# Storing loaded keys and values from SBUF instead of copying them from HBM to HBM, and building the constant masks on chip

## The chip, the cores and the metric

The kernel runs on one core of a Trainium2 chip. The metric is the device time of one launch in microseconds (us), as the median of several runs. The engines are TensorE (PE; its weight loads are shown as PEld), VectorE (DVE), ScalarE (ACT), GpSimd (POOL) and SyncE (SP). All DMA work is issued from the instruction streams of SP (DMA queue q1) and ACT (queue q10), and both queues run on the same 16 DMA engines.

## The reference, cut to what matters

One decoder layer with two parallel mixers: dilated window attention (8 heads of 64) and a gated convolution of width 3. It runs on 512 prompt tokens and on 64 sample tokens (8 sequences of 8), the latter with a cache of 2048 past keys and values per sequence.

```python
proj = jnp.einsum('btd,de->bte', x, w_in)            # 1024 -> 4096
q, k, v, g_att, gb, gc, hh, g_conv = jnp.split(proj, ...)
k_all = jnp.concatenate([k_past, k], axis=1)         # same for v
# three branches (window, dilation): (128,1), (512,4), (2048,16), merged by their softmax sums
att = o_att * jax.nn.silu(g_att)
u = gc * hh
z = gb * conv3(u) * jax.nn.silu(g_conv)
out = jnp.einsum('bte,ed->btd', concat([att, z]), w_out)
y = _layer_norm(2 ** 0.25 * x + out, ln_g, ln_b)
new_k = k_all[:, n_all - keep:]                      # same for v: the caches are outputs too
```

So the kernel returns y and, beside it, the whole key and value caches, shifted by 8 positions. The shift is done outside; the kernel must bring every cached key and value from its input tensor to an output tensor. Of 2048 cached positions of a sequence 1280 are used by some branch ("used": `k_used`, `v_used`), the other 768 are only handed on ("rest": `k_rest`, `v_rest`).

## The kernel before

All matrix products run on TensorE in fp32r, each product in three passes: the weights and the activations are split into a high and a low part (`w_hi`, `w_lo`, `x_hi`, `x_lo`). ACT makes the high part (`split_hi`, L497), DVE the low part (`split_lo`, L810).

The projection has 32 weight tiles of 128 output features (numbers 0 to 31). A tile is projected in two halves, 256 tokens into the bank `pj_a` and 320 into `pj_b` (L1178 to L1180, 24 matmuls each). Tiles 0 and 1 arrive with the input. Tile n from 2 on is loaded by SP (`load_w`, 512 KB in rows of 4 KB) into one of two slots of `w_raw`; the load waits until DVE has split tile n - 2.

Work goes in four rounds, i = 0 to 3, one for each pair of heads. A round has eight tiles (the last has five): C, H, B and G_CONV of the convolution, then V of the next pair, a gate, and q and k of the next pair. Between the tiles stands the attention of pair i: for the prompt, scores (L1282), mask on DVE (L879), exp on ACT (L603), normalisation (L894), transposes on PE (L1299), copies out of PSUM by ACT (`move_prompt`, L609), products with the values (L1313). For the samples, the same with the used keys from `k_buf` (four slots of 1280 KB, rows of 10 KB, loaded by `load_k`, read by PE at L1333) and the used values from `v_buf` (five slots of 1024 KB, rows of 8 KB, `load_v`, read at L1367). After the rounds comes the output projection (L1492 to L1526) and the layer norm.

Every engine runs an instruction stream written out by hand, in order, with semaphore waits. The ones that matter here:

- SP: `load_w`, `load_k`, `load_v`, `save_v`, `save_k` in a fixed order. In round 0 the order is `load_k(0, 2)`, `load_k(0, 3)`, `save_k(0)`, `load_w(6)`, `load_v(0, 0)`, `load_w(7)`, `load_v(0, 1)`, `load_v(0, 2)`, `load_w(8)`, and so on. Tile 6 is the tile B of round 0.
- ACT: `act_round(i)`. Between its computations stand calls of `copy_next()`. Each issues one copy from HBM to HBM: first the 24 pieces of the rest, then 17 pieces of the used values, then the 16 pieces of the used keys, 57 in all. `short_runs` gives them rows of 4 KB (rest and values) or 5 KB (keys), and 256 rows each. None of them waits for anything.
- SP also stores three pieces of the used values of the last round from `v_buf` (`store_values`, L407), since they are there when the engine has time.
- DVE: `dve_round(i)`. In each round `split_lo` of the tile t0 + 3 (tile 6 in round 0) stands ahead of the last two taps of the convolution and of the third prompt mask.

The masks (`mask_pr`, 128 x 512, and `mask_s`, 128 x 1344) are constants that are loaded whole at the start. `w_out` is loaded into SBUF space that `k_buf`, `v_buf` and the small attention buffers have used before (`load_wo`, in the last round), and so are the residual rows `x_res` (`load_res`).

Of the kernel before, what the change touches and what calls it, by code (L numbers as in the profile page):

```python
# [7 lines left out]
P = 128  # L8
D_MODEL = 1024
SEQ = 512  # L10
# [19 lines left out]
NPAIR = DEC_BATCH // 2  # L30
# [10 lines left out]
S_COLS = USED + NS  # L41
K_PIECES = 4
# [5 lines left out]
N_COPIES = 2 * REST_ROWS + NPAIR * (K_PIECES + V_LOADS) - len(STORED)  # L48
# [31 lines left out]
SAMPLE_AT = 3  # L80
Y_SLOTS = 3
# [12 lines left out]
def layer_step(nc, d):  # L94

    with ExitStack() as ctx:
# [68 lines left out]
        v_in = [sem(f"v_in{n}") for n in range(V_LOADS)]  # L165
        k_saved, v_saved, vn_saved, copied, conv_out = (
# [3 lines left out]
        blank = sem("blank")  # L170
# [118 lines left out]

        block = ctx.enter_context(nc.Block())  # L290

        @block.sync
        def _(sp):
# [93 lines left out]
            sp.wait_ge(k_used, pieces + 2)  # L387
            load_wo(1)
            load_v(NPAIR - 1, 3)
            sp.wait_ge(k_used, pieces + 3)  # L390
            load_wo(2)
            load_v(NPAIR - 1, 4)
            sp.wait_ge(k_used, pieces + 4)
            load_wo(3)
# [55 lines left out]
            sp.wait_ge(copied, 16 * N_COPIES)  # L450
            sp.wait_ge(v_stored, 16 * len(STORED))

        @block.gpsimd
        def _(pool):
            pool.memset(q_bd[:, :], 0.0).then_inc(zeroed, 1)
            pool.memset(u_pad[:, 0:2], 0.0).then_inc(zeroed, 1)
            pool.wait_ge(zeroed, 2)
            pool.wait_ge(small_in, 80)
# [24 lines left out]
            pool.wait_ge(ln_in, 16)  # L483
            pool.partition_broadcast(ln_g[:, :], y_t[0:1, 0:D_MODEL]).then_inc(ln_spread, 1)
            pool.partition_broadcast(ln_b[:, :], y_t[0:1, D_MODEL:2 * D_MODEL]).then_inc(ln_spread, 1)

        @block.scalar
        def _(act):
# [44 lines left out]
            def copy_v(i, s):  # L533
                rows = slice((V_LOADS * i + s) * P, (V_LOADS * i + s + 1) * P)
                act.dma_start(short_runs(d["v_used_out"][rows, :]), short_runs(d["v_used"][rows, :]))\
                    .then_inc(copied, 16)

            copies = iter(range(N_COPIES))

            def copy_next():  # L540

                n = next(copies)
                if n < 2 * REST_ROWS:
                    copy_rest(n)
                elif n < N_COPIES - NPAIR * K_PIECES:
                    n -= 2 * REST_ROWS
                    copy_v(n // (V_LOADS), n % (V_LOADS))
                else:
                    n -= N_COPIES - NPAIR * K_PIECES
                    copy_k(n // K_PIECES, n % K_PIECES)  # L550
# [127 lines left out]
            def act_round(i):  # L678
                t0 = tile0(i)
                copy_c(i, 0)  # L680
                copy_next()
# [25 lines left out]
                copy_next()  # L707
                if i == 1:
                    copy_next()
# [5 lines left out]
                copy_next()  # L715
# [6 lines left out]
                copy_next()  # L722
# [3 lines left out]
                copy_next()  # L726
                split_hi(t0 + 9)
                out_sample(i)

            def act_last_round(i):  # L730
                t0 = tile0(i)
                copy_c(i, 0)
                copy_next()
                out_sample_turned(i - 1)
                exp_prompt(i, 0)
                copy_c(i, 1)
                move_prompt(i, 0)
                exp_prompt(i, 1)
                split_hi(t0 + 2)
                move_prompt(i, 1)  # L740
                exp_prompt(i, 2)
                split_hi(t0 + 3)
                copy_next()
                move_prompt(i, 2)
                exp_sample(i)
                split_hi(t0 + 4)
# [3 lines left out]
                copy_next()  # L750
# [19 lines left out]
                copy_next()  # L770
                out_sample(i)
                copy_next()
                copy_next()
                split_mix(2)
                copy_next()
# [11 lines left out]
            for t in range(QT + 1):  # L787
# [8 lines left out]
                if t < 3:  # L796
                    copy_next()
# [6 lines left out]
        def _(dve):  # L804
# [66 lines left out]
            dve.wait_ge(small_in, 80)  # L871
# [301 lines left out]
        def _(pe):  # L1173
# [16 lines left out]
            def turn_v(i):  # L1190

                if i == 0:
                    pe.wait_ge(pj_read[0], 2)
                    pe.wait_ge(small_in, 80)
# [345 lines left out]
def mask_arrays():  # L1540
# [14 lines left out]
    return dict(zip(("mask_s", "mask_pr"), scaled))  # L1555
# [92 lines left out]
```

## Time and profile before

| | |
|---|---|
| median of 3 runs | 354.2 us (353.83 to 355.38) |
| the profiled execution | 354.37 us |
| its span, from the first to the last instruction | 352.6 us |
| PE busy | 343.4 us, 97% of the span |
| DVE, ACT, POOL busy | 201.1, 117.1, 10.9 us |
| DMA | 141.03 MB, 400 GB/s in the mean |
| HBM read, written | 132.66 MB, 71.86 MB |

The span is one profiled execution; 1.8 us of its time lie outside of the span. Busy time of PE is modelled, so whether PE waits is read from the view of waits and from the starts of its matmuls. The packets of the DMA section are rows plus small semaphore writes (16 to each DMA); shares of it are shares of all 16 DMA engines.

### The profile page before, as it was taken

The page shows a single profiled execution, that of the slowest core. Times are in us where ns is not written, and L with a number is a line of the kernel's source. Part 1 is how long each engine was busy: PE and PEld are TensorE (multiplying, and loading weights), DVE is VectorE, ACT ScalarE, POOL GpSimd, SP SyncE. Part 2 cuts the span into 40 slices and gives each one's busy share as a digit, 9 for nine tenths or more (in the row PEclk, how much of TensorE's full clock was granted, in tenths as well). Part 3 has the DMA queues.
Part 4 walks back from the last instruction along what each step waited for, and adds up shares of the span by engine and source line. Part 5 has one row for each costly group of instructions (what it writes and reads, how often), then busy time and mean ns, then how long its engine had stood idle before and what let it go on. Part 6 is the DMA issues. An engine that isn't in the chain of part 4 may idle for free.

```text
span 352.6 us, 7188 instructions
## 1 busy us (share of the span) xinstructions
PE 343.4 (97%) x3024; PEld 297.6 (84%) x3024; DVE 201.1 (57%) x381; ACT 117.1 (33%) x233; POOL 10.9 (3%) x28
## 2 busy tenths in 40 slices
PE   8999999999999999999999999999999999999991
PEld 6998887998889889988898899888888877888791
DVE  3734518955144658651346486613546699794774
ACT  5623324342144333421442425213433644310100
POOL 0000000000100000001000000010000000200000
PEclk9999999999999999999999999999999999999997
DMA  7999999999999999999999999999999999999996
GB/s 295 401 425 416 415 422 418 423 423 418 424 411 423 423 418 410 362 417 418 414 414 422 422 409 341 418 415 404 425 416 418 418 405 342 364 399 385 396 355 256
DMA packets 31570, 141.03 MB, mean 400 GB/s; under 512 B 3121, under 2 KB 3505, under 8 KB 26545
## 3 DMA queue, kind: packets, MB, share of 16 engines
q1 hardware_dynamic: 15890, 76.34, 53.1%
q10 hardware_dynamic: 15648, 64.23, 46.7%
q8 instruction: 24, 0.39, 0.4%
q14 instruction: 8, 0.07, 0.0%
HBM read 132.66 MB, written 71.86 MB: 580 GB/s over the span
## 4 chain that ended last, share of the span: by engine, by line
PE 81%; DMA 9%; DVE 5%; ACT 2%; issue 1%; ACTq 0%; DVEq 0%
PE pj_b L1178 9%; DMA w_raw<-in_w_tiles 9%; PE pj_b L1180 8%; PE pj_b L1179 8%; PE pj_a L1178 7%; PE pj_a L1179 6%; PE pj_a L1180 6%; PE sc L1367 4%; PE sc L1333 4%; PE px L1524 3%; PE px L1526 3%; PE px L1525 3%; PE po L1313 2%; PE px L1282 2%; PE pt L1299 2%; DVE rg L917 1%
## 5 line engine op out<-in xcount | busy, mean ns | idle before, releaser
L1178 PE MATMUL pj_b<-x_hi,w_hi 128*128 128x320 f32 x248 | 78.5, 317 | 0.3 <-DVE mix L933 0.3
L1180 PE MATMUL pj_b<-x_hi,w_lo 128*128 128x320 f32 x248 | 76.5, 309 | 0.0
L1179 PE MATMUL pj_b<-x_lo,w_hi 128*128 128x320 f32 x248 | 76.5, 308 | 0.0
L1178 PE MATMUL pj_a<-x_hi,w_hi 128*128 128x256 f32 (+1 forms) x248 | 71.5, 288 | 0.0
L1180 PE MATMUL pj_a<-x_hi,w_lo 128*128 128x256 f32 (+1 forms) x248 | 69.4, 280 | 0.0
L1179 PE MATMUL pj_a<-x_lo,w_hi 128*128 128x256 f32 (+1 forms) x248 | 69.3, 280 | 0.0
L810 DVE TENSOR_TENSOR w_lo<-w_raw,w_hi 128x1024 fp32r<-128x1024 f32 x30 | 36.7, 1223 | 27.8 <-ACT w_hi L497 27.8
L1178 PEld LDWEIGHTS pj_a<-x_hi,w_hi 128*128 128x128 f32 x248 | 46.9, 189 | 6.1 <-issue 5.6
L1178 PEld LDWEIGHTS pj_b<-x_hi,w_hi 128*128 128x128 f32 x248 | 46.5, 188 | 5.7 <-issue 4.5
L497 ACT CAST w_hi<-w_raw 128x1024 fp32r<-128x1024 f32 x30 | 31.3, 1045 | 57.8 <-PE pj_b L1180 40.2
L1180 PEld LDWEIGHTS pj_a<-x_hi,w_lo 128*128 128x128 f32 x248 | 46.6, 188 | 0.0
L1179 PEld LDWEIGHTS pj_a<-x_lo,w_hi 128*128 128x128 f32 x248 | 46.6, 188 | 0.0
L1179 PEld LDWEIGHTS pj_b<-x_lo,w_hi 128*128 128x128 f32 x248 | 46.5, 188 | 0.0
L1180 PEld LDWEIGHTS pj_b<-x_hi,w_lo 128*128 128x128 f32 x248 | 46.5, 188 | 0.0
L917 DVE RECIPROCAL rg<-rg 128x256 f32<-128x256 f32 (+1 forms) x16 | 31.2, 1953 | 0.5
L879 DVE CUSTOM_DVE_ANT_0 p_pr<-px,mask_pr 128x512 f32<-128x512 f32 (+3 forms) x32 | 14.1, 488 | 14.4 <-PE px L1282 14.4
L603 ACT ACTIVATE p_pr<-p_pr,stat 128x512 f32<-128x512 f32 (+3 forms) x32 | 17.7, 554 | 13.6 <-DVE stat L879 13.6
L1333 PE MATMUL sc<-k_buf,q_bd 128*32 128x320 f32 x256 | 20.3, 435 | 0.2 <-DVE stat L904 0.2
L1367 PE MATMUL sc<-v_buf,pt_s 128*32 128x256 f32 x320 | 19.3, 382 | 0.0
L609 ACT COPY pt_pr<-pt 128x384 f32<-128x384 f32 (+1 forms) x24 | 11.2, 517 | 15.5 <-PE pt L1299 15.4
L862 DVE COPY qk<-pj_b 128x320 f32<-128x320 f32 x4 | 2.0, 492 | 24.3 <-PE pj_b L1180 24.3
L1367 PEld LDWEIGHTS sc<-v_buf,pt_s 128*32 128x32 f32 x320 | 9.4, 109 | 7.0 <-issue 1.8
(169 smaller groups left out, 457.5 us busy)
## 6 DMA issues: line engine op xcount, KB each, us to landing
k_buf<-in_k_used SPq DMA_DIRECT2D x16, 1280.0 KB, 13.4
v_buf<-in_v_used SPq DMA_DIRECT2D x20, 1024.0 KB, 14.1
out_k_used_out<-in_k_used ACTq DMA_DIRECT2D x16, 1280.0 KB, 20.9
out_v_used_out<-in_v_used ACTq DMA_DIRECT2D x17, 1024.0 KB, 15.6
w_raw<-in_w_tiles SPq DMA_DIRECT2D x30, 512.0 KB, 9.9
out_k_rest_out<-in_k_rest ACTq DMA_DIRECT2D x12, 1024.0 KB, 13.9
out_v_rest_out<-in_v_rest ACTq DMA_DIRECT2D x12, 1024.0 KB, 14.8
wo_raw<-in_w_out SPq DMA_DIRECT2D x8, 512.0 KB, 13.1
```

What stands on the lines that cost most here:

```text
L497: nc.scalar.copy(w_hi[:, c], w_raw[:, c]).then_inc(w_hi_done, 1)
L603: nc.scalar.activation(p, p, ACT.Exp, bias=negmax_pr[:, st:st + 1], scale=-1.0, accum_out=sum_pr[:, st:st + 1]).then_inc(pr_exp, 1)
L609: nc.scalar.copy(pt_pr[:, e * SEQ:e * SEQ + step_width(s)], pt[e][:, 0:step_width(s)])\
L810: nc.vector.tensor_tensor(w_lo[:, c], w_raw[:, c], w_hi[:, c].bitcast(F32), ALU.subtract)\
L879: nc.vector.tensor_tensor_reduce(out=p_pr[:, e * SEQ + c0:e * SEQ + c1], in0=px[e][:, c0:c1], in1=mask_pr[:, SEQ - width(u):], scale=-SCAL ...
L917: nc.vector.reciprocal(rg[:, c], rg[:, c]).then_inc(g_step, 1)
L1178: nc.tensor.matmul(out, w_hi[:, w], x_hi[:, c], start=(k == 0), stop=False)
L1179: nc.tensor.matmul(out, w_hi[:, w], x_lo[:, c], start=False, stop=False)
L1180: return nc.tensor.matmul(out, w_lo[:, w], x_hi[:, c], start=False, stop=(k == KT - 1))
L1333: last = nc.tensor.matmul(sc[r * 32:r * 32 + 32, 0:K_COLS], q, k_buf[:, k0:k0 + K_COLS], start=(b == 0), stop=(b == 1 and not ends), skip_ ...
L1367: last = nc.tensor.matmul(sc[r * 32:r * 32 + 32, 0:2 * P], pt_s[:, t * P + r * 32:t * P + r * 32 + 32], v_buf[:, v0:v0 + 2 * P], start=(t ...
L1524: nc.tensor.matmul(out, m_hi, wo[:, hi], start=(n == 0), stop=False)
```

## The change

It does four things.

1. The used keys and values no longer go from HBM to HBM. After a piece has been loaded into `k_buf` or `v_buf`, ACT waits for that load's semaphore and stores the piece from SBUF (`store_k`, `store_v`), in 128 rows of 10 KB or 8 KB. Only the 24 pieces of the rest are left to `copy_next()`.
2. Loading a slot again waits for the store out of it (`k_out`, `v_out`), on SP. So do the loads that take over this space (`load_wo`, `load_res`).
3. The places of the DMAs in ACT's stream are rearranged: a round has four stores of keys, five of values and three copies of the rest.
4. Of the masks only the parts that differ are loaded (128 x 256, 128 x 280 and 128 x 320 instead of 128 x 512 and 128 x 1344); POOL spreads the repeating parts with three copies before its first work of round 0.

```diff
             def load_k / load_v (SP)
                 if i:
                     sp.wait_ge(k_used, n - K_PIECES + 1)
+                    sp.wait_ge(k_out[c], 16 * i)
...
                     sp.wait_ge(v_used, V_PIECES * (i - 1) + 2 * m + 2)
+                    sp.wait_ge(v_out[m], 16 * i)
...
-            for tensor, name in ((ident, "ident"), (mask_pr, "mask_pr"), (state, "state"), (conv_w, "conv_w")):
+            for tensor, name in ((ident, "ident"), (state, "state"), (conv_w, "conv_w")):
                 sp.dma_start(tensor[:, :], d[name]).then_inc(small_in, 16)
-            sp.dma_start(mask_s[:, :], d["mask_s"]).then_inc(small_in, 16)
+            sp.dma_start(mask_pr[:, FAR:], d["mask_pr"]).then_inc(small_in, 16)
+            sp.dma_start(p_s[:, 0:M_COLS], d["mask_parts"]).then_inc(small_in, 16)
+            sp.dma_start(mask_s[:, 8 * P:], d["mask_s"]).then_inc(small_in, 16)
...
             sp.wait_ge(k_used, pieces + 1)
+            sp.wait_ge(k_out[0], 16 * NPAIR)
             load_wo(0)            # the same for k_out[1..3] and load_wo(1..3)
...
             def load_res(t):
+                if t:
+                    sp.wait_ge(v_out[(t - 1) // 2], 16 * NPAIR)
...
         def _(pool):
+            pool.tensor_copy(mask_pr[:, 0:FAR].rearrange("p (n c) -> p n c", c=PATTERN),
+                             repeated(p_s[:, 8:8 + PATTERN], [[0, FAR // PATTERN], [1, PATTERN]])).then_inc(masks_made, 1)
+            old_new = mask_s[:, 0:8 * P].rearrange("p (r n) -> p r n", n=P)
+            pool.tensor_copy(old_new[:, :, 0:OLD], repeated(p_s[:, 0:8], [[1, 8], [0, OLD]])).then_inc(masks_made, 1)
+            pool.tensor_copy(old_new[:, :, OLD:], p_s[:, 8 + PATTERN:M_COLS].rearrange("p (r n) -> p r n", r=8))\
+                .then_inc(masks_made, 1)
...
-            def copy_k(i, c):
-                rows = slice((K_PIECES * i + c) * P, (K_PIECES * i + c + 1) * P)
-                act.dma_start(short_runs(d["k_used_out"][rows, :]), short_runs(d["k_used"][rows, :]))\
-                    .then_inc(copied, 16)
+            def store_k(i, c):
+                n = K_PIECES * i + c
+                act.wait_ge(k_in[c], 16 * (i + 1))
+                act.dma_start(d["k_used_out"][n * P:(n + 1) * P, :], k_buf[:, c * K_SLOT:(c + 1) * K_SLOT])\
+                    .then_inc(k_out[c], 16)
+            def store_v(i, m):      # in place of copy_v, the same with v_in, v_buf and v_out
...
             def act_round(i):
                 copy_c(i, 0)
-                copy_next()
+                store_k(i, 2 if i else 0)
                 if i:
                     out_sample_turned(i - 1)
                 exp_prompt(i, 0)
                 copy_c(i, 1)
                 split_hi(t0 + 2)
-                copy_next()
+                store_k(i, 3 if i else 1)
                 move_prompt(i, 0)
-                if i:
-                    copy_next()
+                if i == 0:
+                    store_k(i, 2)
                 exp_prompt(i, 1)
                 split_hi(t0 + 3)
                 move_prompt(i, 1)
-                copy_next()
+                if i == 0:
+                    store_k(i, 3)
+                store_v(i, 0)
                 exp_prompt(i, 2)
                 split_hi(t0 + 4)
-                copy_next()
-                if i == 1:
-                    copy_next()
+                store_v(i, 1)
                 exp_gate(t0 + G_CONV, 0)
                 move_prompt(i, 2)
-                copy_next()
+                store_v(i, 2)
                 exp_gate(t0 + G_CONV, 1)
                 split_hi(t0 + 5)
                 exp_sample(i)
                 stage_v(i + 1)
-                copy_next()
-                if i == 1:
-                    copy_next()
+                store_v(i, 3)
                 split_hi(t0 + 6)
                 copy_next()
                 out_prompt(i)
                 exp_gate(gate_tile(i), 0)
                 rows_v(i + 1)
-                copy_next()
+                store_v(i, 4)
                 move_sample(i, 0)
                 move_sample(i, 1)
                 exp_gate(gate_tile(i), 1)
                 split_hi(t0 + 7)
                 move_sample(i, 2)
                 copy_q(i + 1)
-                copy_next()
+                store_k(i + 1, 0)
                 split_hi(t0 + 8)
                 copy_next()
                 copy_kk(i + 1)
-                copy_next()
+                store_k(i + 1, 1)
                 split_hi(t0 + 9)
                 out_sample(i)
+                copy_next()
             def act_last_round(i):
                 copy_c(i, 0)
-                copy_next()
+                store_k(i, 2)
                 out_sample_turned(i - 1)
                 exp_prompt(i, 0)
                 copy_c(i, 1)
+                store_k(i, 3)
                 move_prompt(i, 0)
...
```

In the last round `store_v(3, 0)` and `store_v(3, 1)` follow, with nine copies of the rest spread between the computations; two more stand in the layer norm. Before round 0 the four first copies of the rest are issued as they were.

## Rows read from the trace of the kernel before

**Rows 1.** The page: the span.

```profile
span 352.6 us, 7188 instructions
```

**Rows 2.** Busy time in a stretch: window, PE busy (count), clock, DMA share, GB/s.

```profile
12.00:340.00 328.00, 327.33 (x2933) 1.00 1.02 407
```

**Rows 3.** Waits of PE: engine line, releaser: total us, times, longest.

```profile
PE pj_b L1178 <- DVE mix L933: 0.3, 1, 0.3
PE pt L1299 <- DVE p_pr L894: 0.2, 1, 0.2
```

**Rows 4.** The chain that ended last, stretch 36 to 66: start, length, what.

```profile
29.41 21.27 DMA w_raw<-in_w_tiles
...
51.78 1.23 DVE w_lo L810
...
58.72 0.87 PE pt L1299 x6
```

**Rows 5.** Timeline of round 0: start, length, engine, line.

```profile
30.12 0.69 DVE L879 CUSTOM_DVE_ANT_0 p_pr<-px,mask_pr 128x512 f32<-128x512 f32 x1 [0.74 <-PE px L1282]
...
38.09 1.07 ACT L609 COPY pt_pr<-pt 128x512 f32<-128x512 f32 x2 [0.32 <-PE pt L1299]
...
51.65 0.85 ACT L609 COPY pt_pr<-pt 128x384 f32<-128x384 f32 x2
...
53.23 0.86 PE L1313 MATMUL po<-pt_pr,v_rows 128*32 128x128 f32 x24
```

**Rows 6.** DMA queues, stretch 182.5 to 188.7: packets, MB, share of 16 engines.

```profile
q1 hardware_dynamic: 281, 1.53, 59.5%
q10 hardware_dynamic: 281, 1.08, 42.5%
```

**Rows 7.** DMA queues, stretch 39.1 to 50.3.

```profile
q1 hardware_dynamic: 525, 2.80, 60.1%
q10 hardware_dynamic: 488, 1.89, 41.2%
```

**Rows 8.** DMA queues, whole span, and (last line) q1 from 308.5 to 311.5.

```profile
q1 hardware_dynamic: 15890, 76.34, 53.1%
q10 hardware_dynamic: 15648, 64.23, 46.7%
...
q1 hardware_dynamic: 108, 0.74, 58.8%
```

**Rows 9.** DMA issues of round 0: 23.1 to 24, 19.8 to 20; KB, us to landing.

```profile
k_buf<-in_k_used SPq DMA_DIRECT2D x2, 1280.0 KB, 20.7
...
out_v_rest_out<-in_v_rest ACTq DMA_DIRECT2D x1, 1024.0 KB, 19.6
```

**Rows 10.** DMA issues at 61.2 to 61.4 and 234.3 to 234.5.

```profile
v_buf<-in_v_used SPq DMA_DIRECT2D x1, 1024.0 KB, 13.5
...
k_buf<-in_k_used SPq DMA_DIRECT2D x1, 1280.0 KB, 15.1
```

**Rows 11.** DMA issue of `mask_s`, whole span: KB, us to landing.

```profile
mask_s<-in_mask_s SPq DMA_DIRECT2D x1, 672.0 KB, 9.8
```

**Rows 12.** Groups of POOL: count, busy us, mean ns, idle before.

```profile
L471 POOL COPY u_pad<-state 128x16 f32<-128x16 f32 x4 | 3.9, 966 | 0.2
L467 POOL COPY q_bd<-qk 64x64 f32<-64x64 f32 x8 | 1.9, 232 | 152.2 <-DVE qk L856 152.0
```

**Rows 13.** Timeline, places of the stores in round 0 and the last round.

```profile
75.90 1.08 ACT L631 COPY pt_s<-pt 128x512 f32<-128x512 f32 x2
...
79.48 0.38 PE L1353 MATMUL pt<-ident,p_s 128*128 128x128 f32 x2
...
250.41 1.07 ACT L609 COPY pt_pr<-pt 128x512 f32<-128x512 f32 x2
...
252.69 1.06 PE L1313 MATMUL po<-pt_pr,v_rows 128*32 128x128 f32 x32
```

**Rows 14.** Waits of SP at the end: line, releaser: total us, times, longest.

```profile
SPq L450 <- DMA out_k_used_out<-in_k_used: 1.7, 1, 1.7
```

More of the change, by code:

```diff
@@ L41 @@
 S_COLS = USED + NS
+OLD = 3 * P // 4
+FAR = SEQ - 2 * P
+PATTERN = 16
+M_NEAR = 8 * (P - OLD)
+M_COLS = 8 + PATTERN + M_NEAR
 K_PIECES = 4
@@ L47 @@
 STORED = (2, 3, 4)
-N_COPIES = 2 * REST_ROWS + NPAIR * (K_PIECES + V_LOADS) - len(STORED)
+N_REST = 2 * REST_ROWS
 QT = SEQ // P
@@ L80 @@
 SAMPLE_AT = 3
+SMALL = 6 * 16
 Y_SLOTS = 3
@@ L165, in layer_step @@
         v_in = [sem(f"v_in{n}") for n in range(V_LOADS)]
+        k_out = [sem(f"k_out{c}") for c in range(K_PIECES)]
+        v_out = [sem(f"v_out{m}") for m in range(V_LOADS)]
         k_saved, v_saved, vn_saved, copied, conv_out = (
@@ L169, in layer_step @@
         y_out = [sem(f"y_out{n}") for n in range(Y_SLOTS)]
-        blank = sem("blank")
+        blank, masks_made = sem("blank"), sem("masks_made")
         x_hi_done, x_lo_done = sem("x_hi_done"), sem("x_lo_done")
@@ L288, in diagonal_ap, with repeated @@
             return bass.AP(tensor=a.tensor, offset=a.offset, ap=[[512, 64], [32, NPAIR], [P + 16, 2], [1, 8]])
+        def repeated(a, columns):
+            return bass.AP(tensor=a.tensor, offset=a.offset, ap=[[S_COLS, P]] + columns)
         block = ctx.enter_context(nc.Block())
@@ L387, in _ @@
             sp.wait_ge(k_used, pieces + 2)
+            sp.wait_ge(k_out[1], 16 * NPAIR)
             load_wo(1)
@@ L390, in _ @@
             sp.wait_ge(k_used, pieces + 3)
+            sp.wait_ge(k_out[2], 16 * NPAIR)
             load_wo(2)
@@ L393, in _ @@
             sp.wait_ge(k_used, pieces + 4)
+            sp.wait_ge(k_out[3], 16 * NPAIR)
             load_wo(3)
@@ L449, in _ @@
             sp.wait_ge(conv_out, 16)
-            sp.wait_ge(copied, 16 * N_COPIES)
+            sp.wait_ge(copied, 16 * N_REST)
+            for c in range(K_PIECES):
+                sp.wait_ge(k_out[c], 16 * NPAIR)
+            for m in range(V_LOADS):
+                sp.wait_ge(v_out[m], 16 * (NPAIR - (m in STORED)))
             sp.wait_ge(v_stored, 16 * len(STORED))
@@ L457, in _ @@
             pool.wait_ge(zeroed, 2)
-            pool.wait_ge(small_in, 80)
+            pool.wait_ge(small_in, SMALL)
+            pool.tensor_copy(mask_pr[:, 0:FAR].rearrange("p (n c) -> p n c", c=PATTERN),
[4 more added lines that the diff above has]
+                .then_inc(masks_made, 1)
             for i in range(NPAIR):
@@ L526, in copy_rest @@
                 act.dma_start(short_runs(d[name + "_out"][rows, :]), short_runs(d[name][rows, :])).then_inc(copied, 16)
-            def copy_k(i, c):
-                rows = slice((K_PIECES * i + c) * P, (K_PIECES * i + c + 1) * P)
-                act.dma_start(short_runs(d["k_used_out"][rows, :]), short_runs(d["k_used"][rows, :]))\
-                    .then_inc(copied, 16)
[L533 to L538, printed above, removed]
-            def copy_next():
[L542 to L550, printed above, removed]
+            def store_k(i, c):
[4 more added lines that the diff above has]
+            def store_v(i, m):
+                n = V_LOADS * i + m
+                act.wait_ge(v_in[m], 16 * (i + 1))
+                act.dma_start(d["v_used_out"][n * P:(n + 1) * P, :], v_buf[:, m * 2048:(m + 1) * 2048])\
+                    .then_inc(v_out[m], 16)
+            copies = iter(range(N_REST))
+            def copy_next():
+                copy_rest(next(copies))
             def stage_v(i):
@@ L739, in act_last_round @@
                 split_hi(t0 + 2)
+                copy_next()
                 move_prompt(i, 1)
@@ L742, in act_last_round @@
                 split_hi(t0 + 3)
-                copy_next()
+                store_v(i, 0)
                 move_prompt(i, 2)
                 exp_sample(i)
+                copy_next()
                 split_hi(t0 + 4)
@@ L749, in act_last_round @@
                 move_sample(i, 1)
-                copy_next()
+                store_v(i, 1)
                 split_wo(0)
@@ L769, in act_last_round @@
                 split_wo(7)
-                copy_next()
                 out_sample(i)
                 copy_next()
-                copy_next()
                 split_mix(2)
-                copy_next()
                 copy_next()
@@ L795, in _ @@
                 nc.scalar.activation(std[0:rows, :], rstd[0:rows, :], ACT.Sqrt).then_inc(ln_sqrt, 1)
-                if t < 3:
+                if t < 2:
                     copy_next()
@@ L870, in _ @@
             split_lo(4)
-            dve.wait_ge(small_in, 80)
+            dve.wait_ge(small_in, SMALL)
+            dve.wait_ge(masks_made, 3)
             def mask_prompt(i, s):
@@ L1193, in turn_v @@
                     pe.wait_ge(pj_read[0], 2)
-                    pe.wait_ge(small_in, 80)
+                    pe.wait_ge(small_in, SMALL)
                 else:
@@ L1554, in mask_arrays @@
     scaled = [np.maximum(m / SCALE, NEG).astype(np.float32) for m in (np.concatenate([mask_s, new], 1), mask_pr)]
-    return dict(zip(("mask_s", "mask_pr"), scaled))
+    used, near = scaled
+    old = used[:, 0:8 * P].reshape(P, 8, P)
+    assert (old[:, :, 0:OLD] == old[:, :, 0:1]).all()
+    assert (near[:, 0:FAR].reshape(P, -1, PATTERN) == near[:, None, 0:PATTERN]).all()
+    parts = np.concatenate([old[:, :, 0], near[:, 0:PATTERN], old[:, :, OLD:].reshape(P, M_NEAR)], 1)
+    return {"mask_parts": parts, "mask_s": used[:, 8 * P:], "mask_pr": near[:, FAR:]}
 def split_cache(c):
```

## The prediction

> **What bounds the kernel now.** I read the page first, then the busy time of PE over the long middle of the run, then the waits of PE, then the chain that ended last, and the DMA section by queue. The span is 352.6 us [rows 1]. Between 12 and 340 us PE is busy for 327.33 of 328 us at full clock, and in the same stretch the 16 DMA engines have a share of 1.02, which is all there is [rows 2]. PE waits for other engines in three places after its start, the longest for 0.3 us [rows 3]. So PE bounds the kernel. The change takes no matmul away, and what it can win is limited to those waits and to the end of the run. What it can lose is anything that makes PE wait, and the DMA engines are just as full as PE.
>
> One place shows how close the two are. In round 0 the weights of tile 6 are issued at 29.41 and land 21.27 us later, at 50.7; ACT and DVE split the tile (DVE starts at 51.78), DVE goes on to the convolution taps and the third prompt mask, and at 58.72 PE starts the transposes for which it has just waited 0.2 us [rows 3, 4]. That chain from landing to transposes has no slack. Neither has the other branch of it: ACT's copies behind that split start at 51.65 and end at 52.5, and PE uses them at 53.23, 0.7 us later [rows 5]. Whatever delays the landing of tile 6 delays PE by nearly as much, and PE has no idle time later in which to win it back.
>
> **What decides when tile 6 lands.** Both queues run on the same engines. From 182.5 to 188.7 us, with both loaded, each handled 281 packets, though SP's packets were larger: 1.53 against 1.08 MB [rows 6]. From 39.1 to 50.3 us it was 525 against 488 packets, 2.80 against 1.89 MB [rows 7]. So the queues take turns by packet, and a queue's share of the bytes goes with the length of its rows. The short rows of the copies are what lets SP's loads pass them. Stores in rows of 10 KB take that away: against a weight load with 4 KB rows they get 10/14 of the bytes and not half.
>
> The Trainium skill (DMA: Bandwidth & Descriptors, Queues, rings and completion order) says that an engine drains a whole packet of some 9 to 17 descriptors from one ring before it turns to the next. By that rule one of ACT's 17-descriptor copies would have gone for each of SP's 9-descriptor loads, nearly 2 to 1 in counts; the 281 to 281 speaks against it. What it would make of the time is a rival below.
>
> **The change, part by part.**
>
> Stores in round 0, on the path. The fourth copy of the rest is issued at 19.9 and lands 19.6 us later, at 39.5 [rows 9]; up to here ACT's queue is as before. Behind it stood two copies of the rest, of 256 rows of 4 KB. Now there stand store_k(0, 0), store_k(0, 1) and store_k(0, 2). The third is reached after the copies that end at 39.2 [rows 5], and waits for its piece, the first of two issued between 23 and 24 with 20.7 us to landing in the mean; by this ACT reaches it at 41 to 44, while two stores are still in its queue. That is 3 x 128 rows and 48 semaphore writes, 432 packets, against the 525 that SP still moves up to tile 6 [rows 7, 9]. At one for one all three stores go ahead of tile 6. Their price: from the whole span, a MB of q1 costs 53.1% of 352.6 us over 76.34 MB, 2.45 us; of q10, 46.7% over 64.23 MB, 2.56 us; SP's stores of values out of SBUF, the nearest row to the new stores, 58.8% of 3 us over 0.74 MB, 2.38 us [rows 1, 8]. Three stores are 3.93 MB: 9.4 to 10.1 us, and I take 9.6. What q10 did in their place cost 41.2% of 11.2 us, 4.6 us [rows 7]. So 5.0 us are added ahead of tile 6. If the third store came too late for it, 3.2 us less; if the turns favoured the long rows no more than now, nothing.
>
> Smaller masks. 500 KB less is loaded at the start, 0.51 MB at 2.45 us, so 1.25 us less for DMA engines that are full from then on. ACT's first copies move up by it, and tile 6 with them. One more DMA is issued by SP, in a stretch where its next load waits for PE. The spreading on POOL has no row. 1280 columns at the rate of a 64-column copy of 232 ns make 4.6 us; 32 short pieces at 966 / 8 ns, as in the copy of the states, 3.9 us; a memset-like rate below 2 us is the other end [rows 12]. The first mask is used at 30.12 [rows 5], and even the old load of 672 KB, issued among SP's first, took 9.8 us [rows 11]. Some 8 us or more of cover remain; I take 0.
>
> Net at tile 6: 5.0 - 1.25 = 3.75 us later, and PE as much. Bounds: -1.25 (no competition; PE can only use the 0.2 us that it waits) and +4.6 (the dearer price).
>
> Waits on ACT for landings, in all rounds. Behind a store that waits stand ACT's copies out of PSUM, exps and splits, and PE waits for those. Two are the tightest. store_v(0, 4) stands ahead of the sample copies at 75.90, the first of which PE needs at 79.48; its load, issued at 61.3, lands at 74.8 [rows 10, 13]. So the landing may come 4 us later. Round 0 now has six stores of keys, five of values and three copies, 16.3 MB, where there were eleven copies with 11.5: 4.8 MB or 11.8 us more work on full engines, less 1.25, less the 3.75 by which PE is late anyway: up to 6.8 us later. Stall 0 to 2.8, I take 0.3, since ACT itself issues later once it waits. store_k(3, 3) stands ahead of the copies at 250.41, which last 1.07 us and are needed at 252.69; its load, issued at 234.4, lands at 249.5 [rows 10, 13]. 2.1 us may be added. By then the extra work of round 0 has mostly been worked off (rounds 1 and 2 issue 13.6 MB where there were 14.7 and 12.6). Stall 0 to 3, I take 0.2.
>
> Waits on SP for stores. A load of a slot waits for the store out of it, which ACT issued most of a round before. Behind the load stand the weight loads, and PE waits for those. I take 0. The nearest pair is store_k(3, 3) and load_wo(3); if that store is late, it is so for the reason of rival B, and its price is in there.
>
> The end. SP waits 1.7 us for a copy of the used keys [rows 14], which are ACT's last copies now; after the change the last ones are smaller copies of the rest. But the last store of y has to land after that in any case, so only competition with it goes: 0 to half of that wait, -0.8 us, and I take -0.3.
>
> Sum: 354.37 + 3.75 + 0.3 + 0.2 - 0.3 = 358.3 us for the profiled execution. That one ran 0.2 us above the median of the runs, so 358.1 us.
>
> **Rivals.**
>
> A, the forecast: stores in long rows delay tile 6 and PE stalls once, at 53 to 59 us. 356.2 to 361. Chance 0.57.
>
> B, chained waits: the landings in the rest of round 0 and in the last round slip beyond the slack of ACT's stores, and PE waits there too: 354.2 + 3.75 + 2.8 + 3 = up to 363.8. For it: DMA is full everywhere. Against it: ACT's waits throttle what it issues. 361 to 365. Chance 0.13.
>
> C, no stall: the third store is late, or the queue of ACT turns out no heavier: 0 to 1.8 us, 353.8 to 356. For it speaks that the sum of bytes is the same as before. A form of it is turns by whole transfers: three stores of 1.31 MB in place of three copies of 1.05 would pass ahead of tile 6, 0.79 MB or 1.9 us, less 1.25: 354.9. This is what the skill's rule above comes to, and the packet counts are against it. Chance 0.23, the rule alone 0.05 of it.
>
> D, the other side: cheaper transfers free the DMA engines. If 38.8 MB go down from 2.56 to 2.38 us a MB, 7 us of DMA work are gone, with the masks 8. It decides only if tile 6 lands no later than now, since PE is the bound elsewhere. Then PE gains its 0.5 us of waits [rows 3] and the end 0.8: 352.9, and some of that under 352.4. Chance 0.07 with what lies below.
>
> **Numbers.** About 0.5% can be told from no change. Slower by more than that, above 356.0: A, B and a little of C, 0.71. Faster, below 352.4: 0.05. The rest, 0.24, is no difference. The range 353.8 to 362 leaves out the end of B and the better part of D.
>
> **What would show it.** Right: tile 6 lands near 54.4, PE waits some 3 to 4 us in all between 53 and 63 us and hardly anywhere else; between 40 and 54 the two queues have equal packet counts while q10 moves more MB than q1 does with its weights; PE's later stages are all shifted by the same amount. Wrong: tile 6 lands before 51.5; or PE has waits on ACT at the sample copies or in the last round that are longer than the one in round 0; or the end of the run, from the last matmul on, is shorter by more than 1 us.

## The result, and the profile after

The changed kernel takes 366.9 us (median of 4 runs, 366.3 to 369.2) where the kernel before takes 354.0 (352.8 to 355.4): a ratio of 1.038, interval 1.034 to 1.041. Forecast were 358.1 us and a range of 353.8 to 362. The sign was right, the size was not. The profiled execution took 367.45 us.

The page of the changed kernel: span, granted clock and DMA share in 40 slices, and the queues.

```profile
span 365.7 us, 7227 instructions
...
PEclk9999998999999999999999999999899999999998
DMA  8999999999999999999999999999999999989311
...
q10 hardware_dynamic: 11424, 64.23, 42.6%
```

Against [rows 8] ACT's queue moves the same 64.23 MB in 4,224 fewer packets, and less engine time. DMA work has not grown: the engines run dry in the last three slices. HBM reads fall from 132.66 to 93.35 MB, since the stores read SBUF, but the DMA engines have to move as many bytes as before (140.52 MB for 141.03). So the 13 us are to be sought in the order of the transfers.

PE's waits, to be held against [rows 3]; then its windows: the stretch and its length, busy us (count) of PE, PEld, DVE, ACT and POOL, clock, DMA share, GB/s.

```profile
PE po L1339 <- ACT pt_pr L635: 5.8, 2, 2.9
PE pj_b L1204 <- DVE mix L959: 3.6, 2, 2.5
PE pt L1550 <- DVE x_lo L994: 1.8, 1, 1.8
```

```profile
50.00:60.00 10.00, 6.84 (x64) 4.90 (x64) 4.66 (x14) 2.65 (x6) 0.00 (x0) 0.83 1.02 425
...
240.00:260.00 20.00, 17.75 (x142) 14.44 (x141) 5.53 (x15) 4.90 (x12) 0.00 (x0) 1.00 1.02 421
260.00:280.00 20.00, 19.35 (x227) 16.63 (x228) 11.59 (x34) 8.76 (x22) 0.38 (x2) 0.91 1.02 422
280.00:300.00 20.00, 17.52 (x158) 15.18 (x158) 11.88 (x17) 6.97 (x12) 0.00 (x0) 1.00 1.02 420
```

PE loses time in round 0 and from 240 us on (18.24 of 20 us are busy in 300 to 320, too); from 80 to 240 it never waits. The n-th matmul of one kernel is the n-th of the other, so the difference of their starts says where time is lost (us, positions by the kernel before):

```
matmul that starts at   before 53   53.2   56 to 58   60 to 68   74 to 250   252.7   258   287   305 to the last
after starts later by     -0.3       2.8      4.0        3.5        4.9        8.0    9.5   11.7      13.7
```

Round 0 costs 5.2 us, rounds 1 and 2 nothing, the last round with the start of the output projection 8.8. From the last matmul to the end it is 0.6 us shorter.

**Round 0.** Timeline of the changed kernel: start, length, engine, line, in brackets the idle time before and its releaser.

```profile
54.12 1.04 ACT L529 CAST w_hi<-w_raw 128x1024 fp32r<-128x1024 f32 x1 [9.41 <-DMA w_raw<-in_w_tiles]
...
55.98 1.51 PE L1339 MATMUL po<-pt_pr,v_rows 128*32 128x128 f32 x24 [2.92 <-ACT pt_pr L635]
...
68.72 0.44 ACT L647 ACTIVATE rg<-pj_b 128x320 f32<-128x320 f32 x1 [3.75 <-DMA v_buf<-in_v_used]
```

Tile 6 lands 24.8 us after its issue instead of 21.3 ([rows 4]), at 54.1 instead of 50.7. The queues from 39.1 to 50.3 us, the stretch of [rows 7]:

```profile
q10 hardware_dynamic: 300, 2.73, 57.8%
q1 hardware_dynamic: 307, 2.01, 42.8%
```

Packets are one for one as before, and the bytes go to the long rows: SP gets 2.01 MB where it got 2.80. Two things come on top. The 24 matmuls that took 0.86 us in [rows 5] take 1.51 here: after its wait of 2.9 us PE is granted half the clock (1.2 GHz) from 55.6 to 59.0 us, hence the 0.83 in the window, and 1.2 us more are lost (from 2.8 to 4.0 in the table). And ACT stands 3.75 us at `store_v(0, 2)` with the exp of a gate behind it, which PE feels as 1.4 us at the next tile (from 3.5 to 4.9).

**The last round.** DMA queues from 240 to 285 us, before and after, and then the issues to which it comes (count, KB, median us to landing).

```profile
q1 hardware_dynamic: 2658, 13.00, 70.6%
q10 hardware_dynamic: 1265, 5.69, 30.8%
...
out_k_used_out<-in_k_used ACTq DMA_DIRECT2D x5, 1280.0 KB, 13.4
...
wo_raw<-in_w_out SPq DMA_DIRECT2D x8, 512.0 KB, 13.1
```

```profile
q1 hardware_dynamic: 1927, 9.67, 51.8%
q10 hardware_dynamic: 1630, 9.26, 49.4%
...
wo_raw<-in_w_out SPq DMA_DIRECT2D x8, 512.0 KB, 25.3
out_k_used_out<-k_buf ACTq DMA_DIRECT2D x3, 1280.0 KB, 10.7
out_k_rest_out<-in_k_rest ACTq DMA_DIRECT2D x2, 1024.0 KB, 12.9
out_v_used_out<-v_buf ACTq DMA_DIRECT2D x2, 1024.0 KB, 9.0
...
out_v_rest_out<-in_v_rest ACTq DMA_DIRECT2D x1, 1024.0 KB, 15.7
```

Before, ACT issued five copies in these 45 us, none between 243.8 and 263.9, and the loads had 71% of the engines. Now it issues eight, in longer rows, and the loads have 52%: 3.3 MB less, 7.9 us at the 0.42 MB per us that the engines move. Two chains of the changed kernel show where PE meets this:

```profile
239.31 19.80 DMA k_buf<-in_k_used
259.14 0.34 ACTq L563
259.52 0.18 ACT pt_pr L635
...
280.03 29.64 DMA wo_raw<-in_w_out
309.69 1.06 ACT wo L682
...
318.22 0.47 PE pt L1550
```

The last piece of K lands after 19.8 us (15.1 in [rows 10]), and ACT waits for it with the copies of [rows 13] behind; the last tile of `w_out` takes 29.6 us. Between the two stands a wait for the third tile of `w_out`, which takes 24.7 us (ACT's timeline):

```profile
293.66 1.05 ACT L682 CAST wo<-wo_raw 128x1024 fp32r<-128x1024 f32 x1 [4.70 <-DMA wo_raw<-in_w_out]
...
294.62 0.43 ACT L647 ACTIVATE rg<-pj_b 128x320 f32<-128x320 f32 x1
```

The exp of a gate stands behind that wait in ACT's stream, DVE turns it into `mix` by 298.8, and PE goes on then, after 2.5 us (the longer of its two waits for `mix` above). Before the change the same exp waited for PE alone (282.02). So all that is lost from 287 on, 4.2 us, is lost to tiles of `w_out`.

### The profile page after: what moved, and what is told of

Its sections match the earlier page's. It is cut to its first block, busy times and chain, and to the rows that moved or that the text cites. A ratio compares the mean times of both kernels' runs of the same rounds, so it can differ in the third digit from the quotient of the medians.

```text
span 365.7 us, 7227 instructions
## 1 busy us (share of the span) xinstructions
PE 346.2 (95%) x3024; PEld 298.8 (82%) x3024; DVE 202.2 (55%) x381; ACT 115.9 (32%) x233; POOL 15.0 (4%) x31
## 2 busy tenths in 40 slices
DMA packets 27490, 140.52 MB, mean 384 GB/s; under 512 B 3137, under 2 KB 3905, under 8 KB 18241
## 3 DMA queue, kind: packets, MB, share of 16 engines
q10 hardware_dynamic: 11424, 64.23, 42.6%
HBM read 93.35 MB, written 71.86 MB: 452 GB/s over the span
## 4 chain that ended last, share of the span: by engine, by line
PE 66%; DMA 25%; DVE 5%; ACT 1%; SPq 1%; ACTq 1%; issue 0%; DVEq 0%
DMA wo_raw<-in_w_out 8%; DMA v_buf<-in_v_used 8%; PE pj_b L1204 7%; PE pj_b L1206 7%; PE pj_b L1205 7%; PE pj_a L1204 6%; PE pj_a L1205 5%; PE pj_a L1206 5%; DMA k_buf<-in_k_used 5%; DMA w_raw<-in_w_tiles 4%; PE sc L1393 3%; PE sc L1359 3%; PE po L1339 2%; PE px L1550 2%; PE px L1552 2%; PE px L1308 2%
## 5 line engine op out<-in xcount | busy, mean ns | idle before, releaser
L1339 PE MATMUL po<-pt_pr,v_rows 128*32 128x128 f32 x320 | 12.7, 301 | 5.8 <-ACT pt_pr L635 5.8
L1339 PEld LDWEIGHTS po<-pt_pr,v_rows 128*32 128x32 f32 x320 | 9.1, 119 | 8.8 <-ACT pt_pr L635 6.7
## 6 DMA issues: line engine op xcount, KB each, us to landing
w_raw<-in_w_tiles SPq DMA_DIRECT2D x30, 512.0 KB, 13.4
out_v_rest_out<-in_v_rest ACTq DMA_DIRECT2D x12, 1024.0 KB, 13.4
```

The costliest lines, as they stand in the source:

```text
L1339: last = nc.tensor.matmul(po[f * 32:f * 32 + 32, t * P:(t + 1) * P], v_rows[:, v:v + 32], pt_pr[:, c:c + P], start=(k == 0), stop=(k == t))
```

## The experiments

All ratios are to the kernel before, measured together with the experiment. How late PE is, where a DMA lands and what is lost in a round are read from one profiled execution each. Six questions: the copies' path, row length, the masks, how much is handed in early, the single waits, and what else stands on ACT's queue.

**1. From HBM, as before, in short rows, waiting for nothing (`e1_hbm_short`).**

```diff
-                act.wait_ge(k_in[c], 16 * (i + 1))
-                act.dma_start(d["k_used_out"][rows, :], k_buf[...]).then_inc(k_out[c], 16)
+                act.dma_start(short_runs(d["k_used_out"][rows, :]), short_runs(d["k_used"][rows, :])).then_inc(copied, 16)
```

The same for V, and SP's waits for the stores are gone.

> The changed kernel, with every store of used keys and values put back to a copy from HBM to HBM in 256 short rows (5 and 4 KB), without a wait for the load; places and order in ACT's stream as in the changed kernel, new masks kept. Theory L (long rows take the engines' turns from the loads): 353 to 357 us. Rival P (the new places hand in 4.8 MB more in round 0 and some 8 MB more by the last round, and that alone makes loads late): 362 to 368 us, as the changed kernel. Rival W (ACT's waits for landings are what costs): 353 to 358 us, no way to tell it from L here.

359.2 us, 1.012 [1.008, 1.016]. That is above the 353 to 357 of theory L and below the 362 to 368 of rival P: what is handed in early explains at most the 1.2% that are left. In the profiled execution, one of the faster of ten (357.3 us of 356.7 to 361.5), tile 6 lands at 51.7; PE is 1.3 us late behind round 0 and 3.5 at its last matmul.

**2. The same without `short_runs` (`e2_hbm_long`).**

> As the kernel with HBM copies in short rows and no wait, but each copy in 128 rows of 10 or 8 KB. Theory L: 359 to 366 us, with tile 6 landing at 53 us or later; what ACT's own waits cost on top is missing. Rival P: 362 to 368. Rival W: 353 to 358 us.

376.1 us, 1.059 [1.052, 1.065], above every expectation: 4.6% between kernels that differ in nothing but the shape of the rows. The rows came out longer than meant. ACT's queue over the whole span, then both from 39.1 to 50.3:

```profile
q10 hardware_dynamic: 7984, 64.23, 43.0%
...
q1 hardware_dynamic: 268, 2.38, 54.4%
q10 hardware_dynamic: 74, 2.21, 47.7%
```

Rows that follow each other on both sides were joined: the trace has 512 packets of 40 KB and 272 of 64 KB. So this is a kernel with rows far longer than the change's, and it also says how far one for one goes: with rows of 5 KB the counts in this stretch are 465 and 469 (experiment 1), with 10 KB 307 and 300, with 40 and 64 KB 268 and 74. (With 2.5 KB, in experiment 8, they are 588 and 593.)

**3. The change with its stores cut into two runs per row, 5 and 4 KB (`e3_sbuf_short`).**

```diff
+            def in_halves(rows):
+                n = rows.shape[1]
+                return bass.AP(tensor=rows.tensor, offset=rows.offset, ap=[[n // 2, P], [P * n // 2, 2], [1, n // 2]])
...
-                act.dma_start(d["k_used_out"][n * P:(n + 1) * P, :], k_buf[...])
+                act.dma_start(in_halves(d["k_used_out"][n * P:(n + 1) * P, :]), k_buf[...].rearrange("p (m n) -> p m n", m=2))
```

V's stores are cut in the same way, also the three that SP issues in the last round (384 more packets on q1).

> The changed kernel with each store out of SBUF cut into 256 rows of 5 or 4 KB (the output tensor holds the halves of the rows apart); waits and places unchanged. Theory L: 354 to 359 us, and equal packet counts of the queues with q10 at 40% of the bytes. Rival W (waits on landings) and rival P: 363 to 368 us.

358.6 us, 1.012 [1.004, 1.020]. Bytes, path, waits and places are those of the change, and what is lost is 3.9 us instead of 12.9. Tile 6 lands at 51.7. ACT's waits for landings alone do not make the loss. What they cost here (ACT's timeline; the next one, at 67.1, is of 2.70 us, and PE loses 2.0 us up to the tile behind):

```profile
63.26 0.39 ACT L655 ACTIVATE rg<-pj_a 128x256 f32<-128x256 f32 x1 [3.56 <-DMA v_buf<-in_v_used]
```

**4. The new masks in the kernel before (`e4_masks_only`).** The edit is the diff's part on masks.

> The kernel before with the new masks alone. All theories: 352.5 to 354.2 us; tile 6 lands 0.5 to 1.3 us earlier than in the kernel before, and PE can use at most its 0.7 us of waits. If the spreading on POOL held up round 0, it would be 355 or more.

355.9 us, 1.001 [0.998, 1.005]; tile 6 lands at 50.9 and no matmul is more than 0.3 us off. Neither a gain nor a loss. POOL's three spreading copies take 2.6 us in all, from 16.1 us on, and the first mask is used at 30.4: they are hidden.

**5. Experiment 3 with round 0's three copies of the rest moved to rounds 1 and 2 (`e5_short_paced`).**

```diff
-                copy_next()
+                if i:
+                    copy_next()
```

> Stores out of SBUF in rows of 5 and 4 KB, as in the last kernel of that kind, and the three copies of the rest of round 0 put into rounds 1 and 2, so that round 0 hands in 13.1 MB and not 16.3. If what is left over the kernel before (1.2%) is the amount handed in early: 354 to 356.5 us, with PE's first wait of round 0 gone or under 0.5 us and a later tile 7 or 8 no more in the way. If it is ACT's waits for landings: 357 to 359 us, no change.

359.6 us, 1.010 [1.008, 1.013], and 5.8 us late at the last matmul against 4.4. What round 0 hands in is not what remains.

**6. Short rows in the first pair only (`e6_round0_short`).** In both stores, `if i == 0:` ahead of the cut.

> The changed kernel with rows of 5 and 4 KB for the nine stores of pair 0 alone, all later stores in long rows. If the long rows cost in each place by themselves: round 0 gives back 1.5 to 3.5 us and the last round keeps its 8 to 9 us, 362.5 to 365.5 us. If the loss of the last round were a carry-over from round 0: 355 to 361 us.

367.2 us, 1.032 [1.029, 1.034]. Behind round 0 PE is 3.0 us late instead of 4.9, at the last matmul 13.4 where it was 13.7. The last round makes its own loss, whatever round 0 leaves, and a larger one (10.4 us for 8.8): what is gained in round 0 is lost again there, and the run is no shorter than the changed kernel's 366.9.

**7. The change with `store_k(3, 3)` moved behind `split_hi(t0 + 2)` (`e7_k33_later`).**

```diff
                 copy_c(i, 1)
-                store_k(i, 3)
                 move_prompt(i, 0)
                 exp_prompt(i, 1)
                 split_hi(t0 + 2)
+                store_k(i, 3)
```

> The changed kernel with store_k(3, 3) moved behind split_hi(t0 + 2) of the last round, so that ACT's copies for PE no longer stand behind that wait. If this wait alone made the wait of PE at the first values of the last round: 4 to 5 us less there, 361.5 to 363.5 us. If PE would have met the late loads a little later in any case (the keys of piece 3, or w_out at the output projection): 363.5 to 367 us.

367.7 us, 1.033 [1.030, 1.036]. The wait is gone and another stands in for it, by ACT's split of a weight tile (PE's wait, then the chain):

```profile
PE pt L1379 <- ACT pt_s L657: 5.4, 1, 5.4
```

```profile
261.30 24.45 DMA w_raw<-in_w_tiles
...
285.78 0.02 ACT w_hi L529
```

A wait that is only where a late load first shows is not removed by moving the instruction that waits.

**8. Four runs per row, 2.5 and 2 KB (`e8_quarter_rows`).** Experiment 3 with 4 for 2.

> Stores out of SBUF in four runs a row, 2.5 and 2 KB; all else as in the changed kernel. If a queue's share follows its row length all the way down: q10 gets 1/3 of the bytes against 4 KB weight rows, tile 6 lands at 50 us or earlier, and the kernel takes 353.5 to 357 us. If only rows above some length hurt, it is like the rows of 5 and 4 KB: 357 to 360 us. Against it works that short rows cost more of the engines' time, so that the last copies may end after y; then 358 us or more, with PE's waits gone.

366.9 us, 1.031 [1.028, 1.033]. That is above both expectations. The profiled execution is the fastest of five, 363.0 us; the others took 366.5 to 367.0, so some 4 us of the loss stand in no trace. Tile 6 lands at 48.1, earlier than before the change, and PE's wait there is gone. But ACT is held by its own issues (timeline, issuing instructions), and PE waits up to 5.0 us for its copies:

```profile
56.99 8.61 ACTq L576 DMA_DIRECT2D out_v_used_out<-v_buf  x1
65.72 5.04 ACTq L576 DMA_DIRECT2D out_v_used_out<-v_buf  x1
...
259.84 7.66 ACTq L560 DMA_DIRECT2D out_v_rest_out<-in_v_rest  x1
```

Most issues take 0.3 to 0.6 us. The first two of these DMAs have 512 rows, the third 256, and 256 rows are held in other kernels too: up to 5.3 us before the change (at 296.1 us) and 4.9 in experiment 1. In the changed kernel, with the fewest rows, no issue takes over 0.8 us.

**9. Short rows in the last pair only (`e9_last_short`).** In both stores, `if i == NPAIR - 1:` ahead of the cut.

> The changed kernel with two runs per row (5 and 4 KB) only for the stores of the last pair (four of K, two of V); the other pairs keep rows of 10 and 8 KB, and the output keeps the two runs of the last pair's rows apart. Theory A (the share that the loads' queue gets in the last round goes by the row length of the stores beside it): round 0's 5 us stay, of the 8.8 us of the last round at least half comes back, since the waits for tile of W_out and for store_k(3,3) shorten: 359 to 363 us. Theory B (the last round is late because of what round 0 to 2 left undone in the queues): no change, 366 to 368 us.

362.7 us, 1.024 [1.021, 1.026]. PE is still 5.2 us late behind round 0, and the last round adds 3.5 instead of 8.8. So 5.3 of its 8.8 are row length.

**10. Experiment 3 with two stores of V in round 0 later (`e10_short_v_later`).**

```diff
                 split_hi(t0 + 5)
+                if i == 0:
+                    store_v(i, 1)
                 exp_sample(i)
+                if i == 0:
+                    store_v(i, 2)
```

> All stores in two runs per row (5 and 4 KB) as before in the short-row kernel (358.6 us, 1.2% slower than the kernel before), and in round 0 store_v(0,1) behind split_hi(t0 + 5), store_v(0,2) behind exp_sample. Theory A (ScalarE's wait for the landing of V's pieces in front of the gates makes the 1.9 us that tile V loses there): that step goes, 356.5 to 357 us. Theory B (the pieces of V only land when the queues let them, and the gate's place is taken by another wait, for a tile of w): 358 to 359 us.

358.3 us, 1.011 [1.008, 1.013]. PE is now 0.6 us late behind round 0 instead of 3.2, as theory A said, but 4.2 are lost between 287 and 305, and the time is that of theory B: what is gained in one place is lost in the other.

**11. The changed kernel, long rows, with the last round's first three copies of the rest later (`e11_rest_later`).**

```diff
                 split_hi(t0 + 2)
-                copy_next()
...
                 exp_sample(i)
-                copy_next()
...
                 move_sample(i, 2)
-                copy_next()
...
                 split_mix(3)
+                copy_next()
...
                 split_mix(4)
                 copy_next()
+                copy_next()
...
-                if t < 2:
+                if t < 3:
```

> The changed kernel (rows of 10 and 8 KB) with the first three copies of the rest in the last round moved behind the splits of mix and the first norms. Theory A (the last round loses because the loads' queue needs 73.6% of the engines there, as in the kernel before, and gets 57.7%): with 3 MB less on ScalarE's queue up to W_out's last load, 3 MB at 0.42 MB per us are 7 us less, and 4 to 7 of the 8.8 us come back: 360 to 363 us. Theory B (the waits of ScalarE for the landings of K's and V's pieces make the loss by themselves): 366 to 368 us.

360.8 us, 1.019 [1.016, 1.021]. The last round costs 2.2 us, all at `store_k(3, 3)`. The amount on ACT's queue counts like the row length. Queues from 250 to 285, the changed kernel, then this one:

```profile
q1 hardware_dynamic: 1499, 8.01, 55.1%
q10 hardware_dynamic: 1198, 6.73, 46.2%
```

```profile
q1 hardware_dynamic: 1817, 9.73, 67.0%
q10 hardware_dynamic: 745, 4.96, 33.9%
```

**12. Experiments 10 and 11 together (`e12_all_short_later`).**

> All three together: two runs per row, V's stores of round 0 later, the last round's first three copies of the rest later. If the parts add up: round 0 leaves 1.3 to 1.5 us, the last round nothing, so 355.5 to 356.5 us against 354 to 355 before. If what is left of the short-row kernel's 1.2% comes from the sum of the transfers and not from their order: 358 us.

357.8 us, 1.011 [1.008, 1.014], not the 355.5 to 356.5 of the sum. 3.1 us are lost at 301 to 304.5, the start of the output projection. The two longest of four such waits of SP, ahead of its loads of `w_out` (the others are 5.3 and 5.2 us):

```profile
SPq L409 <- DMA out_k_used_out<-k_buf: 11.0, 1, 11.0
...
SPq L405 <- DMA out_k_used_out<-k_buf: 6.7, 1, 6.7
```

The loads of `w_out` go where K's pieces were, and wait for the stores out of them. The last of these lands 31.5 us after its issue at 250.5; in the changed kernel it was 10.5 us.

**13. Experiment 12 with the last two copies of round 2 later as well (`e13_short_five_later`).** In `act_round`, `if i < NPAIR - 2:` ahead of its last two `copy_next()`; two more of them between the splits of `mix` and the first norm.

> The kernel with two runs per row, V's stores of round 0 later and the last round's first three copies of the rest later (357.8 us, 3.5 us late at its last matmul, 3.1 of them at 301 to 304.5 us), and the last two copies of the rest of round 2 (issued at 232 and 241.5 us) moved behind the splits of mix too. Theory A (SyncE's loads of W_out wait for the stores of the last K pieces, 11.0, 6.7, 5.3 and 5.2 us, and those stand behind the copies of the rest in ScalarE's queue): the stores land sooner, the 3.1 us go, the last matmul is 0.5 to 1 us late, 355 us against 354.4 before. Theory B (the loads of W_out are late because all engines are full, whoever has the packets): 357.5 us as without this move.

354.9 us, 1.003 [1.002, 1.005]. The longest waits of PE that are left (the first is the one at the start, which is there before the change too):

```profile
PE sc L1250 <- DVE rg L848: 1.3, 1, 1.3
PE sc L1377 <- DVE stat L948: 0.9, 1, 0.9
```

1.0 us is lost in round 0, most of it in the second row, scores behind DVE's work on tile 6, and nothing afterwards. This is the best version with the stores out of SBUF, and it does not beat the kernel before.

**14. The changed kernel, long rows, with the same five copies later (`e14_long_five_later`).**

> The changed kernel (rows of 10 and 8 KB, stores where the change has them) with the last two copies of round 2 and the first three of the last round moved behind the splits of mix. With the latter three alone it took 360.8 us, with 4.6 us lost in round 0 and 2.2 at ScalarE's wait for store_k(3,3)'s piece (252.7 us). Theory A (that piece lands late because the copies of the rest at 232 and 241 us share the engines with its load): the 2.2 us go, 358 to 359 us. Theory B (it lands late since long-row stores of K take the share, copies or not): 360 to 361 us.

358.7 us, 1.013 [1.010, 1.015]. The last round costs nothing. (The copies that the expectation puts at 232 and 241 us were issued at 236.3 and 245.6 in experiment 11.) `load_k(3, 3)` shows why (issues of 239 to 250 us, experiment 11, then this one), and ACT no longer waits for its landing:

```profile
k_buf<-in_k_used SPq DMA_DIRECT2D x1, 1280.0 KB, 18.9
```

```profile
k_buf<-in_k_used SPq DMA_DIRECT2D x1, 1280.0 KB, 16.2
```

With the long rows in place, moving five copies gives back 8.2 us. What is left are the 4.7 us of round 0.

## Why the prediction was right in direction and wrong in size

- **What bounds the kernel, and the mechanism: right.** PE had no slack, turns go packet for packet at these row lengths, and long rows on ACT's queue delay SP's loads. Experiment 3 takes the rows back, and 3.9 us are lost instead of 12.9; experiment 9 does so in the last pair, and PE is 8.7 us late at its last matmul instead of 13.7. In experiment 6 the rows of round 0 give time back there, and the last round takes it again.
- **Tile 6 later by 3.75 us, landing near 54.4: right, in part by luck.** The third store is issued at 43.0 and lands at 53.1, ahead of tile 6, as forecast. Tile 6 lands at 54.1, 3.4 us later than before, and PE is 3.8 us later behind it (from -0.3 to 3.5 in the table). That is the forecast's number by another sum: PE waits 2.9 us, the half clock takes 1.2 more, and 0.5 come back right behind it. Since the masks' 1.25 us did not show (experiment 4), the 5.0 us for the stores were too much, by about as much. No row of the kernel before showed a wait that long in its middle.
- **`store_v(0, 4)`, 0 to 2.8 us, 0.3 taken: inside the bounds, over the term, and the place wrong.** ACT's wait that hurt was the one at `store_v(0, 2)`, 1.4 us; experiment 10 removes its like.
- **The last round, 0.2 us taken: this is the step that failed.** The prediction said that by then the extra work has mostly been worked off. Its own numbers don't say so: rounds 1 and 2 hand in 27.2 MB where there were 27.3, so next to nothing of round 0's 4.8 MB is made up for. And the last round itself was never counted: eight issues by ACT where there were five in the 45 us in which SP must load `w_out`, the last V and the last tiles. It cost 8.8 us: 3.1 at `store_k(3, 3)` where 0.2 stood, 1.5 by the half clock behind it, and 4.2 behind `w_out`, 2.2 by its third tile and 2.0 by its last, for which the sum had no term. Of the 9 us by which the profiled execution misses the forecast of 358.3, this is 8.6. Experiments 9, 11 and 14 give back 5.3 us by row length, 6.6 by three copies, and all by five; each is enough for more than half, so the parts don't add up to the sum.
- **Smaller masks, -1.25 us: nothing measurable** (experiment 4). The spreading, bounded at 2 to 4.6 us, took 2.6, hidden as forecast. **Waits on SP, 0: right for the change, and wrong once rows are short** (experiment 12).
- **The end, -0.3:** 0.6 shorter from the last matmul on.
- **Rivals.** B had the right places, ACT's stores in round 0 and in the last round, but a stall of at most 3 us there; it argued that ACT's waits throttle what it issues. They did not do so enough: from 240 to 285 us ACT's queue moved 9.26 MB where it had moved 5.69. It was given 0.13. C fell with tile 6, and its turns by whole transfers fall with the counts of experiment 8, 588 to 593 with 512 rows a store against 128 rows a load. D's premise was true: a MB of ACT's queue costs 42.6% of 365.7 us over 64.23 MB, 2.43 us for 2.56 before, 9 us of DMA work in all; half of it is there in experiment 1 too (2.50), with path and rows as before. PE could make nothing of it, since the loads came later. The range ended 5 us too low since the last round's stall was bounded by one landing, not by the share of a whole stage.

It stays open what ACT's waits cost or save by themselves with long rows: experiment 2, which was to show it, also had far longer packets. With short rows, copies from HBM that wait for nothing and stores that wait take the same time (experiments 1 and 3, 1.012 both). That long rows are what makes these losses is shown; that the losses of single places add up is not, since experiments 6, 9, 10 and 11 each shift some of them.

## What to carry to other kernels

With two queues on the same DMA engines, row length is a priority: before a transfer's rows are made longer for efficiency, ask which loads stand beside it, and count for every stage, the last one above all, what each queue has to move there and by when. Transfers that nobody waits for are ballast that can be put anywhere; once stores have to follow landings, the free copies have to move out of the stages where loads are urgent (8.2 us here). A wait found at an engine's in-order instruction is worth moving only if the transfer behind it is not late itself (experiment 7).

## What the runs showed of the hardware

- A wait of 2.9 us of TensorE in the middle of full work was followed by 3.4 us at the half clock, twice in the changed kernel (from 55.6 and from 260.4 us), each worth another 1.2 to 1.5 us. Waits of 2.6 us (experiment 11, with one of 0.9 behind it), 2.4 (experiment 6) and 2.1 (experiment 2) were followed by it too; waits of 2.5 us (changed kernel, at 296.4) and 2.1 us (experiment 10) were not. In experiment 13, where no wait is longer than 1.3 us, there is no such stretch ahead of the end.
- HBM to HBM, rows that are contiguous on both sides are joined to packets of 40 and 64 KB, and then the other queue gets several of its packets for one (268 to 74).
- A KB costs nearly the same in every row length from 2 to 64 KB, 39 to 43 ns of one engine. By the queue's share, rows of 10 and 8 KB cost 2.43 us a MB and 5 and 4 KB 2.46 (experiment 3), 1.6% more; the kernel before and experiment 1, with the same rows and path, differ by more than that (2.56 and 2.50).
- An issue can hold ACT for up to 8.6 us (experiment 8). Counted from the rows issued and the packets moved, every issue of over 1.2 us, there, in experiment 1 and before the change, began with 970 to 1,650 packets of ACT's queue still to be moved; the changed kernel never had more than 500 of them at an issue. Fewer, longer rows are not only a matter of bandwidth.
